# One call moved by one place in VectorE's order: the low part of a spectrum ahead of one low part of weights

## The chip, the cores and the metric

The program runs on one core of one Trainium2 chip. The metric is the device time of one execution in microseconds (us); lower is better. For the kernel before, three timed runs and one profiled execution are shown.

## The reference, cut to what matters

The program computes two transformer-like blocks, one behind the other, on 256 tokens of width 1024, all in fp32. The change lies in the second block, in its Hyena mixer, which convolves a sequence twice with a long filter and gates the result after each convolution:

```python
def long_conv_bidir(u, h_fwd, h_bwd, bias):
    ...
    U = jnp.fft.rfft(u.astype(jnp.float32), n=2 * L, axis=1)
    K = jnp.fft.rfft(k2, n=2 * L, axis=0)
    y = jnp.fft.irfft(U * K[None], n=2 * L, axis=1)[:, :L]
    ...
    for n in range(HY_ORDER):
        z = gates[n] * long_conv_bidir(z, filt[:, 0, n], filt[:, 1, n], bias[n])
```

Beside it stand the gate projections `h @ w_in` (the columns `gna` and `ghy`), which need nothing from the convolution.

## The kernel before, in words

**Numbers in two parts.** TensorE multiplies fp32r tiles. To keep fp32 accuracy, each operand is a high part (ScalarE copies the fp32 value into fp32r) and a low part (VectorE subtracts the high part from the value). A product is then three matmuls: high by high, low by high, high by low. This holds for weights (`wh`, `wl`), for the activations (`xh`, `xl`) and for the convolution's data (`zh`, `zl` ahead of the forward transform, `yh`, `yl` ahead of the inverse one).

**Weights.** All weights come as one stream of chunks of 1 MB, each of two *halves* of eight 128x128 tiles. SyncE loads chunks into three buffers `raw`, in order (`sync_load`, L375). A chunk may be loaded into a buffer only when VectorE has made the low parts of both halves of the chunk that was there; SyncE waits for those in turn. ScalarE makes the high part of a half (`casts`, L430, with `cast`, L420, which waits for the load), VectorE the low part (`rests`, L447, with `rest`, L441). Each of the sixteen gate projections, gate 0 to gate 15, uses one half; the half of gate 0 is the first of its chunk, so gates 6 and 7 share a chunk, 8 and 9 the next, and so on. The load of the chunk of gates 12 and 13 goes into the buffer of gates 6 and 7, so it is issued when gate 7's low part is there. That of gates 14 and 15 follows gate 9's low part, and that of the two halves behind gate 15 follows gate 11's. The high and low parts themselves lie in five slots here: the parts of gate g+5 go where those of gate g were, so ScalarE casts gate 12 behind the tanh of gate 7 (`gate_act`, L2410), and VectorE makes gate 7's low part in `rests(2)`, gate 8's in `rests(3)`, gate 9's in `rests(4)`, gate 10's in `rests(5)`, those of gates 11 and 12 in `rests(7)`.

**The convolution.** The channels go in two halves, (n, 0) and (n, 1), for each of the convolutions n = 0 and 1. One pass of (n, half) is:

- TensorE's forward transform, 12 matmuls (`fwd_pe`, L2462); they need `zl`, and the bank of the first six must have been read by the splitting of the pass before;
- ScalarE copies the odd bank out (`fwd_act`, L2479), and VectorE forms the sum and the difference of the banks (`fwd_split`, L2495);
- VectorE multiplies by the filter's spectrum and adds up (`fwd_products`, L2505; `fwd_sums`, L2516). The last two operations of `fwd_sums` are the two halves `w` of the product's spectrum, in the tile `a`;
- ScalarE makes the high part of each, `yh` (`fwd_high`, L2539), and VectorE the low part, `yl` (`fwd_low`, L2530, two operations; each waits for `w` and for `yh`);
- TensorE's inverse transform, 12 matmuls (`inv_pe`, L2550), which wait for both `yl`;
- for n = 0, VectorE gates the result (`z_next`, L2441), ScalarE and VectorE make its parts (`z_hi`, L2423; `z_lo`, L2432), and the next pass begins. For n = 1, ScalarE copies it out (`inv_act`, L2566) and TensorE transposes it (`hy_back`, L2573).

**The order.** Each engine works its instructions off in the order in which the program issues them; the order is written out by hand, for TensorE in `tail_pe` (L2627), for ScalarE in `tail_act` (L2656) and for VectorE in `tail_dve` (L2709). TensorE's begins

```python
        gate(2, 3, 4)
        self.inv_pe(P, 0, 0)
        gate(5, 6)
        self.inv_pe(P, 0, 1)
        gate(7)
        self.fwd_pe(P, 1, 0)
        gate(8)
        self.fwd_pe(P, 1, 1)
        gate(9, 10, 11)
        self.inv_pe(P, 1, 0)
        gate(12)
        self.hy_back(P, 0)
```

In ScalarE's order, `gate(7)` (the tanh of gate 7 and the cast of gate 12) stands ahead of `fwd_act(A, 1, 0)`.

Of the kernel before, what the change touches and what calls it, by code (L numbers as in the profile page):

```python
# [238 lines left out]
class Kernel:  # L239
# [207 lines left out]
    def rests(self, V, spent, late=False, most=None):  # L447

        W = self.W
        if late:  # L450
            V.spent, spent = spent, V.spent
        V.spent = max(V.spent, spent)
        end = W.halves if most is None else min(W.halves, V.next_half + most)
        while V.next_half < end:
            b = W.before[("half", V.next_half)]
            if b is not None and not (b[1] < spent if b[0] == "half" else b in V.over):
                break
            h = V.next_half
            if not self.on_pool(h):
                self.rest(V, ("half", h), self.S["w_lo"])  # L460
            V.next_half += 1
# [2247 lines left out]
    def tail_dve(self, V):  # L2709
        S, W = self.S, self.W  # L2710
        rests = lambda n: self.rests(V, W.spent(("gate", n)))
        self.fwd_split(V, 0, 1)
        self.fwd_products(V, 0, 1)
        self.fwd_sums(V, 0, 1)
        rests(2)
        self.fwd_low(V, 0, 1)
        self.z_next(V, 0)
        rests(3)
        self.z_lo(V, 1, 0)
        self.z_next(V, 1)  # L2720
        rests(4)
        self.z_lo(V, 1, 1)
        self.fwd_split(V, 1, 0)
        rests(5)
        self.fwd_products(V, 1, 0)
        self.fwd_sums(V, 1, 0)
        rests(7)
        self.fwd_low(V, 1, 0)
        self.fwd_split(V, 1, 1)
        rests(8)  # L2730
        self.fwd_products(V, 1, 1)
        self.rests(V, W.spent(("gate", 10)), most=1)
        self.fwd_sums(V, 1, 1)
        rests(10)
        self.fwd_low(V, 1, 1)
        rests(11)
        self.hy_gated(V, 0)
        rests(12)
        self.hy_lo(V, 0)
        rests(13)  # L2740
        rests(14)
        self.hy_gated(V, 1)
        for k in range(4):
            s = slice(512 * k, 512 * (k + 1))
            if k == 1:
                rests(15)
                self.hy_lo(V, 1)
            V.wait_ge(S["hy_a"], ("gate", 2 * k + 1))
            V.wait_ge(S["proj"], ("nao", 2 * k + 1))
            V.stt(self.SA[:, s], self.SA[:, s], 1.0, self.ps[self.bank[("nao", "twin", k)]][:, :], ALU.add,  # L2750
                  ALU.mult).then_inc(S["hy_v"], ("mna", k))
            if k < 3:
                self.rests(V, W.spent(("nao", 2 * k + 1)))
        V.wait_ge(S["out_a"], ("shift",))
        V.tt(self.pads()[:, :, 1:2], self.mod[:, 24:32].rearrange("p (d c) -> p d c", d=8),
             self.pads()[:, :, 0:1].bitcast(F32), ALU.subtract).then_inc(S["out_v"], ("shift",))

        def lower(k):
            s = slice(512 * k, 512 * (k + 1))
            V.wait_ge(S["hy_a"], ("mh", k))  # L2760
            V.tt(self.ML[:, s], self.merged(k), self.MH[:, s].bitcast(F32), ALU.subtract).then_inc(S["hy_v"], ("ml", k))

        self.rests(V, W.spent(("nao", 7)))
        for k in range(4):
            s, t = slice(512 * k, 512 * (k + 1)), self.merged(k)
            V.wait_ge(S["hy_a"], ("gate", 9 + 2 * k))
            V.wait_ge(S["proj"], ("hyo", 2 * k + 1))
            V.stt(t, self.SH[:, s], 1.0, self.ps[self.bank[("hyo", "twin", k)]][:, :], ALU.add,
                  ALU.mult).then_inc(S["hy_v"], ("mhy", k))
            V.wait_ge(S["hy_v"], ("mhy", k))  # L2770
            V.tt(t, t, self.SA[:, s], ALU.add).then_inc(S["hy_v"], ("m", k))
            if k:
                lower(k - 1)
                self.rests(V, W.spent(("hyo", 2 * k - 1)), most=1 if k == 3 else None)
        lower(3)
        V.over.add(("tail",))
        self.rests(V, W.spent(("hyo", 7)))
        add = lambda d: self.add_x(V, "mod", d, M0, TR, self.ps[self.bank[("out", d)]][:, :TR], ("out", d),
                                   self.small[:, 24 + d:25 + d])
        low = lambda d: self.norm_lo(V, "mod", d, M0, TR, self.small[:, 16 + d:17 + d], 258)  # L2780
        add(0), add(1), low(0), add(2), low(1)
        self.rests(V, W.spent(("out", 0)))
        low(2)
        for d in range(3, DT):
            self.rests(V, W.spent(("out", d - 2)))
            add(d)
            self.rests(V, W.spent(("out", d - 1)))
            low(d)
        self.rests(V, W.spent(("out", 7)))
        self.rsqrt_dve(V, "mod", self.R[1], self.ps[7][:, :TR], TR)  # L2790
# [328 lines left out]
```

## Time and profile before

| | before |
|---|---|
| timed runs, us | 1000.8, 1002.09, 1002.31 (median 1002.09) |
| profiled execution, us | 1005.83 |
| its span in the profile, us | 1004.0 |
| TensorE (PE) busy | 97% of the span |
| VectorE (DVE) busy | 82% |
| ScalarE (ACT) busy | 56% |
| granted TensorE clock, mean | 0.997 of full speed |

Busy time is an average over the whole program. In the stretch that the change touches, from 700 to 760 us, all of TensorE, VectorE and ScalarE depend on one another, so there the single instructions have to be read in order of time: when one starts, whether its engine sat idle ahead of it, and for whom it waited. Starts are counted from the beginning of the span. Two instructions that follow each other on VectorE or ScalarE overlap by about 0.1 us in the records, so the next one starts a little before the first one's end.

### The profile page before, as it was taken

How to read it: one execution, taken by the hardware profiler on the slowest of the kernel's cores; microseconds unless marked ns; L12 is line 12 of the kernel's file. 1: busy time of each engine (PE TensorE's matmuls, PEld its weight loads, DVE VectorE, ACT ScalarE, POOL GpSimd, SP SyncE). 2: the span in 40 equal slices, each digit the busy share in tenths (PEclk: the TensorE clock that was granted, in tenths of full speed). 3: DMA queues.
4: the chain of work that ended last, by engine and by line, in shares of the span. 5: the costliest groups of instructions: out<-in, count | busy, mean ns of one | idle time of the engine just before them, and what ended most of it. 6: DMA issues, size and time to landing. Idle time of an engine off the chain costs nothing.

```text
span 1004.0 us, 19347 instructions
## 1 busy us (share of the span) xinstructions
PE 973.0 (97%) x7884; PEld 951.9 (95%) x7884; DVE 822.7 (82%) x1376; ACT 562.5 (56%) x1051; POOL 102.8 (10%) x128
## 2 busy tenths in 40 slices
PE   7999999999999999999999999999999999999996
PEld 6999999999899989999999998889999999999996
DVE  7999798887999967999969967998998968767443
ACT  6756454445766756555545535666545556655432
POOL 4100000111000003002103301122000100000000
PEclk9999999999999999999999999999999999999998
DMA  9564657665433315998758813443345446555441
GB/s 281 224 253 166 241 200 237 236 232 204 154 141 105 127 63 209 344 324 298 272 173 296 322 52 134 143 142 110 123 165 211 172 154 221 211 170 197 144 162 42
DMA packets 33880, 192.17 MB, mean 191 GB/s; under 512 B 4976, under 2 KB 6272, under 8 KB 15104
## 3 DMA queue, kind: packets, MB, share of 16 engines
q1 hardware_dynamic: 23440, 157.36, 43.6%
q10 hardware_dynamic: 6912, 25.17, 7.4%
q0 software_dynamic: 3440, 8.42, 2.8%
q8 instruction: 62, 1.02, 0.4%
q14 instruction: 26, 0.21, 0.1%
HBM read 187.78 MB, written 3.15 MB: 190 GB/s over the span
## 4 chain that ended last, share of the span: by engine, by line
PE 77%; DVE 13%; ACT 6%; issue 2%; DMA 2%; SPq 0%; DVEq 0%; ACTq 0%
PE ps L93 76%; DVE wl L70 3%; ACT wh L67 2%; PE ps L96 1%; DMA raw<-w 1%; DVE a L70 1%; DVE b L70 1%; ACT u L67 1%; DMA cst<-cst 1%; DVE s L77 1%; DVE c L81 1%; DVE l L73 1%; ACT s L67 1%; DVE natl L70 0%; ACT a L67 0%
## 5 line engine op out<-in xcount | busy, mean ns | idle before, releaser
L70 DVE TENSOR_TENSOR wl<-raw,wh 128x1024 fp32r<-128x1024 f32 x283 | 343.8, 1230 | 16.1 <-ACT wh L67 15.8
L67 ACT ACTIVATE wh<-raw 128x1024 fp32r<-128x1024 f32 x286 | 295.9, 1049 | 23.5 <-PE ps L93 11.2
L93 PE MATMUL ps<-xh,wh 128*128 128x256 f32 (+1 forms) x992 | 279.7, 282 | 1.2 <-DVE xl L73 1.1
L93 PE MATMUL ps<-xh,wl 128*128 128x256 f32 (+1 forms) x992 | 278.5, 281 | 0.0
L93 PE MATMUL ps<-xl,wh 128*128 128x256 f32 x992 | 277.4, 280 | 0.0
L93 PE MATMUL ps<-xt,wh 128*128 128x272 f32 (+1 forms) x1120 | 217.4, 289 | 0.9 <-DVE wl L70 0.7
L93 PEld LDWEIGHTS ps<-xh,wh 128*128 128x128 f32 x992 | 188.2, 190 | 1.7 <-DVE xl L73 1.3
L93 PEld LDWEIGHTS ps<-xl,wh 128*128 128x128 f32 x992 | 187.1, 189 | 0.0
L93 PEld LDWEIGHTS ps<-xh,wl 128*128 128x128 f32 x992 | 186.7, 188 | 0.2
L93 PEld LDWEIGHTS ps<-xt,wh 128*128 128x128 f32 x1120 | 177.2, 188 | 2.2 <-issue 0.8
L93 PE MATMUL ps<-xt,wl 128*128 128x272 f32 (+1 forms) x560 | 160.1, 286 | 0.0
L93 PE MATMUL ps<-hl,wh 128*128 128x256 f32 (+1 forms) x528 | 149.1, 282 | 0.0
L93 PE MATMUL ps<-hh,wh 128*128 128x256 f32 (+1 forms) x528 | 149.0, 282 | 0.0
L93 PE MATMUL ps<-hh,wl 128*128 128x256 f32 (+1 forms) x528 | 149.0, 282 | 0.0
L93 PEld LDWEIGHTS ps<-xt,wl 128*128 128x128 f32 x560 | 105.7, 189 | 0.3
L93 PEld LDWEIGHTS ps<-hl,wh 128*128 128x128 f32 x528 | 100.0, 189 | 0.0
L93 PEld LDWEIGHTS ps<-hh,wh 128*128 128x128 f32 x528 | 99.5, 188 | 0.1
L93 PEld LDWEIGHTS ps<-hh,wl 128*128 128x128 f32 x528 | 99.1, 188 | 0.0
L70 POOL TENSOR_TENSOR acc<-acc,sq 128x256 f32<-128x256 f32 (+1 forms) x30 | 34.0, 1133 | 506.8 <-ACT sq L67 506.8
L67 ACT ACTIVATE hh<-fh 128x256 fp32r<-128x256 f32 (+1 forms) x66 | 27.9, 422 | 102.4 <-DVE fh L70 78.6
L67 ACT ACTIVATE sq<-x 128x256 f32<-128x256 f32 (+1 forms) x43 | 17.5, 417 | 84.3 <-DVE x L70 50.9
L84 DVE CUSTOM_DVE_ANT_0 ada<-ada,cb 128x1024 f32<-128x1024 f32 x42 | 55.9, 1330 | 0.1
(343 smaller groups left out, 1574.8 us busy)
## 6 DMA issues: line engine op xcount, KB each, us to landing
raw<-w SPq DMA_DIRECT2D x141, 1024.0 KB, 5.0
ada<-ada ACTq DMA_DIRECT2D x42, 512.0 KB, 4.5
cb<-ada ACTq DMA_DIRECT2D x6, 512.0 KB, 4.6
raw<-w SPq DMA_DIRECT2D x4, 512.0 KB, 6.5
spare<-w SPq DMA_DIRECT2D x2, 1024.0 KB, 9.3
spectra<-ev POOLq DMA_DIRECT2D x8, 256.0 KB, 3.7
skew<-rpb POOLq DMA_DIRECT2D x8, 192.0 KB, 3.5
x<-x POOLq DMA_DIRECT2D x2, 544.0 KB, 9.1
```

The source lines that it names most:

```text
L67: return Issued(self.e and self.e.activation(out, src, func, **kw))
L70: return Issued(self.e and self.e.tensor_tensor(out, a, b, op))
L73: return Issued(self.e and self.e.scalar_tensor_tensor(out=out, in0=in0, scalar=scalar, in1=in1, op0=op0, op1=op1))
L77: return Issued(self.e and self.e.tensor_scalar(out, src, s1, s2, op0=op0))
L81: return Issued(self.e and self.e.tensor_tensor_scan(out, a, b, 0.0, op0=ALU.add, op1=ALU.bypass))
L84: return Issued(self.e and self.e.tensor_tensor_reduce(out, a, b, scale, start, op0, op1, accum))
L93: return Issued(self.e and self.e.matmul(out, stat, mov, start=start, stop=stop))
L96: return Issued(self.e and self.e.transpose(out, src, ident))
```

## The change

In VectorE's order the two operations of `fwd_low` for (0, 1) are issued ahead of the low part of gate 7's weights instead of behind it. Nothing is added or removed, and no other engine's order changes. The calls that lie around it:

```diff
--- before.py
+++ after.py
@@ -2712,8 +2712,8 @@
         self.fwd_split(V, 0, 1)
         self.fwd_products(V, 0, 1)
         self.fwd_sums(V, 0, 1)
+        self.fwd_low(V, 0, 1)
         rests(2)
-        self.fwd_low(V, 0, 1)
         self.z_next(V, 0)
         rests(3)
         self.z_lo(V, 1, 0)
```

## Rows read from the trace of the kernel before

**Rows 1.** The profile's page, busy us of the engines

```profile
PE 973.0 (97%) x7884; PEld 951.9 (95%) x7884; DVE 822.7 (82%) x1376; ACT 562.5 (56%) x1051; POOL 102.8 (10%) x128
```

**Rows 2.** Waits, 704 to 760 us: us in total, times, longest us

```profile
ACT wh L67 <- DMA raw<-w: 2.7, 1, 2.7
...
PE ps L93 <- DVE yl L70: 0.9, 1, 0.9
...
PE ps L96 <- ACT a L67: 0.6, 1, 0.6
...
PEld ps L93 <- ACT sghy L67: 0.3, 1, 0.3
```

**Rows 3.** Waits of TensorE, 752 to 1004 us

```profile
PE ps L93 <- ACT sq L67: 0.6, 1, 0.6
```

**Rows 4.** The chain that ended last, 727 to 751 us: start, us, what

```profile
727.61 5.79 PE ps L93 x48
...
733.42 0.61 ACT a L67
...
741.72 1.15 DVE wl L70
...
742.93 6.11 DMA raw<-w
...
749.07 0.02 ACT wh L67
...
750.03 0.58 ACT a L67
...
750.75 0.63 PE ps L96 x4
```

**Rows 5.** VectorE in order of time: start, us, instruction, [idle before <-releaser]

```profile
723.92 1.29 DVE L70 TENSOR_TENSOR a<-b 128x512 f32<-128x512 f32 x2
725.13 1.22 DVE L70 TENSOR_TENSOR wl<-raw,wh 128x1024 fp32r<-128x1024 f32 x1
726.26 1.29 DVE L70 TENSOR_TENSOR yl<-a,yh 128x512 fp32r<-128x512 f32 x2
727.47 0.68 DVE L70 TENSOR_TENSOR z<-ps,g 128x512 f32<-128x512 f32 x1
728.07 1.22 DVE L70 TENSOR_TENSOR wl<-raw,wh 128x1024 fp32r<-128x1024 f32 x1
...
734.05 1.42 DVE L70 TENSOR_TENSOR a<-ps,a 128x512 f32<-128x512 f32 x2 [1.83 <-ACT a L67]
```

**Rows 6.** ScalarE in order of time, 724 to 733 us

```profile
725.24 0.63 ACT L67 ACTIVATE yh<-a 128x512 fp32r<-128x512 f32 x1
...
732.06 0.38 ACT L67 ACTIVATE sgna<-ps 128x256 f32<-128x256 f32 x1 [0.91 <-PE ps L93]
732.34 1.05 ACT L67 ACTIVATE wh<-raw 128x1024 fp32r<-128x1024 f32 x1
```

**Rows 7.** TensorE's matmuls and its weight loads (PEld), in order of time

```profile
727.61 0.39 PE L93 MATMUL ps<-yh,gh 128*128 128x256 f32 x1 [0.88 <-DVE yl L70]
...
735.94 0.28 PE L93 MATMUL ps<-zh,fh 128*128 128x256 f32 x1
...
727.60 0.19 PEld L93 LDWEIGHTS ps<-yh,gh 128*128 128x128 f32 x1 [1.07 <-DVE yl L70]
...
729.03 0.19 PEld L93 LDWEIGHTS ps<-xh,wh 128*128 128x128 f32 x1
```

**Rows 8.** SyncE's loads: issues, then us to landing (722:727, 700:765, 600:640, all)

```profile
726.42 0.33 SPq L99 DMA_DIRECT2D raw<-w  x1
...
DMA to landing us min/median/max: 4.8/4.8/4.8
...
DMA to landing us min/median/max: 4.8/4.9/6.1
...
DMA to landing us min/median/max: 4.8/4.8/7.1
...
DMA to landing us min/median/max: 3.4/5.0/11.7
```

## The prediction, made before the changed kernel was run

> **What bounds the kernel now.** I read the page first: TensorE is busy 97% of the span, VectorE 82% [rows 1]. A move on VectorE can only give back time in which TensorE waits for it, so the waits of the stretch come next. From 704 to 760 us TensorE stands three times: 0.9 us for `yl`, 0.3 us at a weight load, and 0.6 us at the transposes (L96) for ScalarE's `a` [rows 2]. From 752 us to the end it waits for 0.6 us in all, in the last norm [rows 3]. So whatever moves the transposes at 750.75 moves the end by as much, and nothing behind them gives it back.
>
> The chain says what moves them [rows 4]. The inverse transform (0, 1) starts at 727.61; 48 matmuls (inverse 12, gate 7 24, forward 12) run to 733.40; ScalarE copies the forward's bank out at 733.42; VectorE works through split, products and sums to gate 11's low part, which ends at 742.87; that frees a buffer, the load issued at 742.93 takes 6.11 us, and ScalarE, in order, casts at 749.07 and only then copies the inverse out at 750.03. Hence two questions: what the move does to 727.61, and whether that reaches 733.42.
>
> VectorE's order shows the part to be moved [rows 5]: the two `w` at 723.92, gate 7's low part at 725.13, the two `yl` at 726.26, `z` at 727.47. The first `yl` could start as soon as its `yh` is there. ScalarE's order shows the second `yh` from 725.24 to 725.87 [rows 6]; the first ends as the second starts, give or take 0.03 us.
>
> **The change, part by part.** *Removed from ahead of `yl`:* one 128x1024 subtraction. The two `w` end at 723.92 + 1.29 = 725.21. Now ScalarE sets the pace. The first `yl` starts at about 725.29. The second waits for the second `yh`, 725.87 + 0.03 (an ACT to DVE release as from 733.42 + 0.61 to 734.05 [rows 4, 5]) = 725.90. With 0.69 us of its own it ends at 726.59, against 726.26 + 1.29 = 727.55 before: 0.96 us earlier. TensorE's matmuls ahead of the inverse run out at 727.61 - 0.88 = 726.73 by the records [rows 7], and the first weight load may go 0.05 us behind `yl`, at 726.64. **The inverse starts 0.96 us earlier** and the wait of 0.9 us is gone.
>
> *Moved behind `yl`:* gate 7's low part. VectorE's start to start for a 128x512 subtraction ahead of another operation is 728.07 - 727.47 = 0.60 us [rows 5], so it starts at 725.90 + 0.60 = 726.50, not 725.13: **1.37 us later**, ending at 727.72. Three things wait for it.
>
> (a) TensorE's gate 7. The inverse takes 729.03 - 727.60 = 1.43 us [rows 7], so gate 7's first weight load comes at 726.64 + 1.43 = 728.07; the low part is there at 727.72 + 0.05. No wait, with 0.3 us to spare.
>
> (b) VectorE itself. The swapped operations fill the same time but for 0.17 us of standing for `yh`: `z` goes from 727.47 to 727.64, and all up to the last `zl` moves by that. The 1.83 us in which VectorE stands at 734.05 [rows 5] covers it.
>
> (c) SyncE. The load of gates 12 and 13 waits for exactly this low part: it was issued at 726.42 [rows 8], 0.07 us behind its end at 725.13 + 1.22 = 726.35. Now: 727.72 + 0.07 = 727.79. This same load took 4.8 us to land [rows 8]: 731.22 before, 1.1 us ahead of the cast of gate 12 at 732.34 [rows 6], and **732.59 after**. TensorE is 0.96 us ahead, so gate 7's tanh comes at about 731.2 and ScalarE would cast gate 12 at 731.5. It has to stand there until 732.59 + 0.03 = 732.62, and the copy of the forward's bank is queued behind. In the chain such a copy starts 750.03 - 749.07 = 0.96 us behind the cast [rows 4]: 732.62 + 0.96 = **733.58, against 733.42. That is 0.16 us later than before**, although TensorE has the bank ready at 732.44. This is the step on which the forecast rests: the gain on TensorE is real and is eaten by a load that the same move delays.
>
> From there on each step repeats the chain, 0.16 us later. VectorE's split moves from 734.05 to 734.21, its end from 735.47 to 735.63. The second forward transform, at 735.94 before [rows 7], is reached at 734.98 but needs the split: 735.68. So here TensorE gives back 0.70 of its 0.96 us. Gate 11's low part ends at 743.03 instead of 742.87; there TensorE stood 0.3 us before [rows 2] and now stands about 0.26 + 0.16 = 0.4 us longer, which gives back the rest. The load behind it goes out at 743.09, and with 6.11 us as before the transposes start at 750.91. What that last load takes is not the change's doing: at the 4.9 us of its neighbours [rows 8] its wait for ScalarE at the transposes would be gone, in either kernel, and gate 11's low part, still 0.16 us later, would set the end.
>
> The sum is -0.96 (inverse) +0.96 (given back at the split and at gate 11) +0.16 (ScalarE's cast behind the load) = **+0.16 us**, on the profiled execution 1005.83 + 0.16 = 1005.99. The timed runs lie 3.7 us below that one; nothing in the term depends on that difference, so it goes on their median: 1002.09 + 0.16 = 1002.25, rounded to 1002.2.
>
> The unknown price is the landing of the delayed load. Each 0.1 us of it is 0.1 us at the end, down to a floor of -0.96, where the cast no longer holds ScalarE (landing 3.7 us and less). Ends from rows: 3.4 us, the shortest of the trace, gives -0.96; 7.1 us, the longest in the stretch from 600 to 640 us, gives +2.46 [rows 8]. I take 4.8, since it is this very load's figure and the smallest and nearly the median of the stretch. Two loads beside it, of 4.9, would make it +0.26.
>
> The Trainium skill (DMA: Bandwidth & Descriptors, section Anatomy of one DMA) fits a DMA that GpSimd issues with about 2.0 us plus its bytes by 436 GB/s. As an estimate from that page, 1 MB lands in 4.4 us, which would make the sum -0.24 us instead of +0.16; the trace's 4.8 decides here, and both are no change.
>
> **The rivals.** *A, the gain stays.* ScalarE is not held by the cast, because the load lands within 3.7 us. Then 733.42 becomes 732.46, the chain moves by -0.96 and so does the end: 1002.09 - 0.96 = 1001.1. For it: TensorE is the busiest engine and its one wait for `yl` goes. Against it: none of the loads from 700 to 765 us landed in under 4.8 us [rows 8].
>
> *B, the load lands late.* It is one mechanism: gates 12 and 13's load, issued 1.37 us later, runs into whatever made the load at 742.93 take 6.11 us [rows 4]. Before, a landing of up to 5.9 us cost nothing (732.34 - 726.42); now each tenth over 4.64 us costs. At 6.1 us it is 4.8's +0.16 plus 1.3: 1003.6. It passes 0.2% (2.0 us, about what a measurement of this kernel can tell from no change) only from 6.65 us of landing; at 7.1 us the time is 1002.09 + 2.46 = 1004.6. For it: one load of eight here took 6.1. Against it: over 6.65 is rare, and it would have to fall on this load in most runs.
>
> *C, the move does nothing.* If the second `yh` came later than reckoned, ScalarE and not VectorE's order would set `yl`, at its old time. For that `yh` would have to be 0.96 us late, and it is on record at 725.24 [rows 6]. Then only the load's delay would be left, +0.16 as well: 1002.2.
>
> **How the numbers follow.** The forecast, between -0.3 and +0.5 us, gets 0.74; rival A, or part of it, 0.10; rival B at 6.1 us or so 0.08, and past 0.2% 0.04; C 0.02; 0.02 is for what I don't see, on either side. All but B's far end and the unseen lie within 0.2% of 1002.09. B's far end and half of the unseen make slower 0.05; the other half, and A where the measurement adds as much again, make faster 0.03; the same gets 0.92. The timed runs of one kernel lie 1.5 us apart, so a median may be off by some 0.5 us: the range goes from A's 1001.1 less 0.5 to B's 1003.6 (its own spread is in the two in ten left out), 1000.6 to 1003.6.
>
> **What would show it.** In the changed kernel's trace: `yl` at about 725.3 and 725.9; no wait of TensorE for `yl`; the load issued at 727.8; a new wait of ScalarE's `wh` for the load of about 1.1 us ahead of 732.6; the copy `a` at 733.6; new waits of TensorE of about 0.7 us near 735 and 0.7 us near 743. The prediction is wrong if that wait of ScalarE's isn't there, or if 733.42 moves by more than 0.4 us either way. If the end moves and 733.42 does not, it is the late load behind gate 11, not the change.

## The result, and the profile after

The changed kernel takes 1004.0 us (median of 19 runs, 1002.01 to 1005.3) against 1001.89 us for the kernel before (19 runs, 1000.49 to 1003.23). The ratio is 1.0019, with a 95% interval of 1.0012 to 1.0025: **1.9 us slower, between 1.2 and 2.5**. Forecast were 1002.2 us and a range from 1000.6 to 1003.6.

The profiled execution of the changed kernel took 1002.4 us, its span is 1000.6 us. That is less than the span of before, and it says nothing: the two executions differ by 3.6 us before they come to the change at all (the last section says where). So times are counted here from a common mark, the start of the first `w` of (0, 1) on VectorE, at 723.92 us before [rows 5] and at 720.31 us after. VectorE of the changed kernel in order of time:

```profile
720.31 1.29 DVE L70 TENSOR_TENSOR a<-b 128x512 f32<-128x512 f32 x2
721.77 1.29 DVE L70 TENSOR_TENSOR yl<-a,yh 128x512 fp32r<-128x512 f32 x2 [0.17 <-ACT yh L67]
722.99 1.22 DVE L70 TENSOR_TENSOR wl<-raw,wh 128x1024 fp32r<-128x1024 f32 x1
724.12 0.68 DVE L70 TENSOR_TENSOR z<-ps,g 128x512 f32<-128x512 f32 x1
...
731.80 1.42 DVE L70 TENSOR_TENSOR a<-ps,a 128x512 f32<-128x512 f32 x2 [2.93 <-ACT a L67]
```

The order is the one meant. `yl` ends at +2.75 instead of +3.63, 0.88 us earlier; gate 7's low part starts at +2.68 instead of +1.21, 1.47 us later. But VectorE then stands 2.93 us for ScalarE's copy `a`, not 1.83 [rows 5]. ScalarE shows why:

```profile
727.71 0.37 ACT L67 ACTIVATE sgna<-ps 128x256 f32<-128x256 f32 x1
730.23 1.06 ACT L67 ACTIVATE wh<-raw 128x1024 fp32r<-128x1024 f32 x1 [2.15 <-DMA raw<-w]
731.20 0.57 ACT L67 ACTIVATE a<-ps 128x512 f32<-128x512 f32 x1
```

The tanh of gate 7 is done at 728.08, and the cast of gate 12 waits 2.15 us for its load. Before, there was nothing to wait for at this place [rows 6]. The copy of the forward's bank stands behind the cast and starts at +10.89 instead of +9.50, 1.39 us later. SyncE in order of time has the load's issue:

```profile
724.28 0.33 SPq L99 DMA_DIRECT2D raw<-w  x1
```

and the view of the tile `raw` what it took to land:

```profile
DMA to landing us min/median/max: 5.9/5.9/5.9
```

It went out at +3.97 instead of +2.50 and took 5.9 us instead of 4.8 [rows 8]. The chain that ended last now runs from gate 7's low part through this load, where before it ran over TensorE [rows 4]:

```profile
723.07 1.15 DVE wl L70
...
724.28 5.92 DMA raw<-w
730.21 0.02 issue
730.23 1.06 ACT wh L67
731.29 0.49 ACT a L67
...
739.47 1.15 DVE wl L70
...
740.68 6.27 DMA raw<-w
...
747.94 0.59 ACT a L67
...
748.66 0.63 PE ps L96 x4
```

From the copy on it is the chain of before, link by link. The transposes come at 748.66 - 720.31 = +28.35, against 750.75 - 723.92 = +26.83: **1.52 us later**, 1.36 from the first load and 0.16 from the second, which took 6.27 us instead of 6.11. The waits of TensorE in the changed kernel (716 to 757 us: us in total, times, longest):

```profile
PE ps L93 <- DVE a L70: 1.7, 1, 1.7
PE ps L96 <- ACT a L67: 0.7, 1, 0.7
PE ps L93 <- DVE wl L70: 0.3, 1, 0.3
```

The 0.9 us for `yl` [rows 2] is gone, and 1.7 us stand in its place, ahead of the second forward transform, whose bank the delayed split has not yet read.

### The profile page after: what moved, and what is told of

It reads as the page before. It is cut to its first block, busy times and chain, and to the rows that moved or that the text cites. A ratio compares the mean times of both kernels' runs of the same rounds, so it can differ in the third digit from the quotient of the medians.

```text
span 1000.6 us, 19347 instructions
## 1 busy us (share of the span) xinstructions
PE 968.3 (97%) x7884; PEld 947.3 (95%) x7884; DVE 822.1 (82%) x1376; ACT 562.7 (56%) x1051; POOL 104.9 (10%) x128
## 3 DMA queue, kind: packets, MB, share of 16 engines
q8 instruction: 62, 1.02, 0.4%
## 4 chain that ended last, share of the span: by engine, by line
PE 76%; DVE 13%; ACT 6%; DMA 2%; issue 2%; SPq 0%; DVEq 0%; ACTq 0%
PE ps L93 75%; DVE wl L70 3%; ACT wh L67 2%; DMA raw<-w 2%; PE ps L96 1%; DVE a L70 1%; DVE b L70 1%; ACT u L67 1%; DVE c L81 1%; DVE s L77 1%; DMA cst<-cst 1%; DVE l L73 1%; ACT s L67 1%; DVE natl L70 0%; DVE s L84 0%
```

## The experiments

T1 is the theory that the loss is the load of gates 12 and 13, delayed by the move, through ScalarE's order. R is the rival that VectorE's new order makes it by itself, C that one long landing was chance. All times with a plus sign count from the first `w` of (0, 1). The table collects what the traces show; "late load" is the one behind gate 11's low part, and a fetch is a packet of 16 KB on the instruction queue q8, in us behind the load's issue ("none": none from the issue to the landing). The last column is the time from the first `w` of (0, 1) to the end of the span; in the two traces marked *, TensorE's pace late in the program was another one (last section), which makes this figure some 1.3 us smaller.

| kernel | load issued | took | fetch | copy | late load took | fetch | transposes | end of span |
|---|---|---|---|---|---|---|---|---|
| before | +2.51 | 4.8 | 4.4 | +9.50 | 6.1 | 1.5 | +26.8 | +280.1 |
| before, again | +2.51 | 4.7 | 4.2 | +9.50 | 6.1 | 3.0 | +26.9 | +280.1 |
| after | +3.97 | 5.9 | 2.5 | +10.9 | 6.3 | 2.9 | +28.4 | +280.3 * |
| after, again | +3.98 | 6.0 | 2.6 | +11.0 | 6.3 | 2.9 | +28.4 | +281.7 |
| after, copy first | +3.97 | 6.1 | 2.7 | +8.63 | 6.0 | 2.9 | +25.9 | +279.1 |
| before, load late | +3.72 | 4.9 | 4.5 | +9.64 | 6.5 | 3.4 | +27.3 | +280.6 |
| before, load later | +5.46 | 4.8 | none | +11.3 | 6.5 | 1.5 | +29.0 | +282.2 |
| after, shifted | +3.97 | 4.9 | none | +9.82 | 4.8 | none | +26.3 | +280.1 |
| before, shifted | +2.50 | 4.8 | none | +9.51 | 4.9 | none | +26.0 | +279.9 |
| after, both first | +3.97 | 6.9 | 2.3 | +8.65 | 6.2 | 2.8 | +25.4 | +277.7 * |
| before, both first | +2.51 | 4.8 | 4.3 | +9.50 | 6.4 | 1.5 | +26.0 | +279.9 |
| after, both first, shifted | +3.97 | 4.7 | none | +8.63 | 4.8 | none | +25.3 | +278.9 |

**The copy ahead of the cast.** In the changed kernel, ScalarE copies the forward's bank out before it casts gate 12:

```diff
-        gate(7)
+        self.gate_act(A, 7, False)
         self.fwd_act(A, 1, 0)
+        self.casts(A, W.spent(("gate", 7)))
```

with `gate_act` making its casts only if its third argument is true.

> The changed kernel with one more move: in ScalarE's order the copy of the forward's bank (fwd_act for (1, 0)) stands ahead of the cast of gate 12. Theory T1 (the loss is the load of gates 12 and 13, issued later, which holds ScalarE at the cast with the copy queued behind): the copy no longer waits for the load and follows TensorE, about 2.3 us earlier than in the changed kernel, so this kernel comes out about 1.0 us faster than the kernel before (1000.9 us against 1001.9) and about 2.5 us faster than the changed one; the wait of ScalarE for the load may stay, but nothing of the chain is behind it. Rival R (the loss is VectorE's own new order: its standing for yh, or gate 7's low part made late): it stays at about 1.9 us slower than before.

Measured: 1000.96 us against 1001.6, ratio 0.9998 (0.9985 to 1.0011). ScalarE in order of time:

```profile
732.10 0.60 ACT L67 ACTIVATE a<-ps 128x512 f32<-128x512 f32 x1 [0.86 <-PE ps L93]
733.53 1.06 ACT L67 ACTIVATE wh<-raw 128x1024 fp32r<-128x1024 f32 x1 [0.84 <-DMA raw<-w]
```

The load took 6.1 us and the cast still waits for it, but the copy now follows TensorE, at +8.63. The transposes are at +25.9, 0.97 us ahead of those of before and 2.5 us ahead of the changed kernel's, and the end of the span is 1.0 us ahead: the whole gain that the move of `yl` makes on TensorE reaches the end as soon as ScalarE's order does not put the load in its way. R falls: it had this kernel 1.9 us slower than before, and the timed runs have it 0.2 us faster, between 1.5 us faster and 1.1 us slower. They alone would not have shown the gain of 1 us, since their interval is 2.6 us wide; that is read from the trace. Of the 0.97 us, 0.88 are TensorE's lead at the second forward transform and 0.09 the late load's, which took 6.02 us instead of 6.11.

**The load alone, late.** The kernel before, VectorE's order untouched, with one more wait of SyncE's:

```diff
+        if x == ("w", 101):
+            D.wait_ge(self.S["hy_v"], ("yl", 0, 1, 1))
```

> The kernel before with one more wait: SyncE issues the load of gates 12 and 13 only when both yl of (0, 1) are there, 1.2 us later than before, with VectorE's order as before. T1: the load lands at about 732.4 us if it takes 4.8 us, which costs nothing, and at about 733.5 if TensorE's instruction fetch falls into it as it did in the changed kernel; then the copy moves from 733.4 to 734.5 and the time by +1.1 us, to 1003.0. R: VectorE's order is that of before, so no change, 1001.9.

Measured: 1001.86 us against 1001.6, ratio 1.0003 (0.9987 to 1.0019). The load took 4.9 us, the copy came at +9.64 and so cost 0.14 us; another 0.4 us at the transposes is the late load's, which took 6.5 us here. It is T1's harmless branch, and thus no proof: R expected as much. The fetch came 4.5 us behind the issue, when the load was all but in. So the same load was held back further, until gate 8's low part:

```diff
+        if x == ("w", 101):
+            D.wait_ge(self.low_signal(198), ("half", 198))
```

> The kernel before with VectorE's order untouched and the load of gates 12 and 13 held back further: SyncE issues it when gate 8's low part is there, at +5.44 instead of +2.51 (times from the start of the first w of (0, 1)). T1 (the load alone, through ScalarE's order, makes the loss): with 4.8 us it lands at +10.2, the copy of the forward's bank moves from +9.5 to +11.2, the transposes from +26.8 to +28.5, and the time is 1.7 us over that of the kernel before; with a fetch in it (6 us) the copy is at +12.4. R (VectorE's new order makes the loss): this order is that of before, so the copy stays at +9.5 and the time at that of before.

Measured: 1004.29 us against 1001.78, ratio **1.0022** (1.0011 to 1.0033). ScalarE in order of time:

```profile
729.11 1.06 ACT L67 ACTIVATE wh<-raw 128x1024 fp32r<-128x1024 f32 x1 [1.76 <-DMA raw<-w]
730.08 0.58 ACT L67 ACTIVATE a<-ps 128x512 f32<-128x512 f32 x1
```

Its load took 4.8 us. The copy is at 730.08 - 718.82 = +11.3, as expected, and the transposes at +29.0, 2.1 us late (1.76 from the copy, 0.4 from the late load's 6.5 us). VectorE's order is that of before. A late load by itself makes the loss of the changed kernel, and more.

**The fetch.** That leaves why the load took 5.9 us. The page has a queue that I had passed over: q8, kind instruction, 62 packets, 1.02 MB. The DMA view of the changed kernel, from the issue to 728.9 us, when the load should have been in:

```profile
DMA packets 142, 1.05 MB, mean 228 GB/s; under 512 B 15, under 2 KB 15, under 8 KB 15
## 3 DMA queue, kind: packets, MB, share of 16 engines
q1 hardware_dynamic: 141, 1.03, 63.2%
q8 instruction: 1, 0.02, 1.3%
```

Each of the 16 engines ends its share of a load with a packet of 4 B. By 728.9 there are 15 of them, and one packet of q8 is among the load's. It takes 1.3% of the 16 engines' 4.6 us, which is 0.96 us, close to the 1.1 us by which this load is longer. The sixteenth comes about 1.1 us behind the others (the view from 729.3 to 730.2 us):

```profile
DMA packets 18, 0.14 MB, mean 155 GB/s; under 512 B 1, under 2 KB 1, under 8 KB 1
```

In the kernel before, the load's data from 726.4 to 730.7 us has no q8 packet beside it:

```profile
q1 hardware_dynamic: 133, 1.05, 71.7%
issues: line engine op xcount, KB each, median us to landing
raw<-w SPq DMA_DIRECT2D x1, 1024.0 KB, 4.8
```

To test it, 60 waits that are long satisfied were put into TensorE's stream, far ahead, where they cost nothing, in either kernel:

```diff
+            if name[:2] == ("up", 1) and P.e is not None and t % 4 == 3 and P.spent < 60:
+                P.spent += 1
+                P.e.wait_ge(self.low_signal(h).sem, self.low_signal(h).at[("half", h)])
+                P.e.wait_ge(self.S["ld_fz"].sem, self.S["ld_fz"].at[("load",)])
```

> The changed kernel with 60 more instructions in TensorE's stream, waits that are long satisfied, spread over the up projections of layer 1, where they cost nothing. They move each of TensorE's instruction fetches of 16 KB behind them about 3.4 us earlier against the work. T1 in its strong form (the load takes 5.9 us because one such fetch, at 726.8 us in the changed kernel's trace, holds one of the 16 DMA engines in the midst of it): the fetch falls ahead of the load, the load lands in 4.8 us, the copy comes 1.1 us earlier than in the changed kernel, and the later load of 6.3 us falls to about 4.9 as well. The time against the same shift of the kernel before is +0.2 us instead of +1.9. If the long landing has another cause, the load still takes 5.9 us and the difference stays at +1.4 to +1.9.

> The kernel before with the same 60 satisfied waits in TensorE's stream: the partner of the shifted changed kernel. T1: the later load, 6.1 us before, lands in 4.8 to 4.9 us, TensorE's wait of 0.6 us at the transposes goes, and the time falls by 0.6 to 0.8 us against the kernel before, to 1001.2. The load of gates 12 and 13 may take 6 us here, which costs nothing since the cast of gate 12 comes 5.9 us behind its issue. If fetches have nothing to do with landings, both loads stay as before and the time too.

Measured: the changed kernel shifted takes 1000.92 us (ratio 0.9992, 0.9981 to 1.0004), the kernel before shifted 1001.66 us (1.0007, 0.9995 to 1.0019), both against 1001.6. ScalarE of the shifted changed kernel, in order of time:

```profile
727.55 1.06 ACT L67 ACTIVATE wh<-raw 128x1024 fp32r<-128x1024 f32 x1 [1.09 <-DMA raw<-w]
728.52 0.58 ACT L67 ACTIVATE a<-ps 128x512 f32<-128x512 f32 x1
```

and the landings of its load of gates 12 and 13 and of the late load:

```profile
DMA to landing us min/median/max: 4.9/4.9/4.9
...
DMA to landing us min/median/max: 4.8/4.8/4.8
```

The fetch next to the first load moved 5.2 us earlier in the changed kernel and 5.8 in the one before, not 3.4. That it moved says whose it is: only TensorE's stream was changed. Their number fits: 62 packets for the 7884 matmuls and 7884 weight loads of the page is one for every 254 of these, so a fetch comes at nearly fixed places of TensorE's stream. Both loads fell, 5.9 to 4.9 and 6.3 to 4.8 us. ScalarE's wait is the 1.09 us that the prediction had. Against its partner the shifted changed kernel is 0.31 us later at the copy and 0.30 at the transposes: the forecast's +0.16, a little larger; at the end of the span it is 0.24 us.

The expectation for the kernel before, 0.6 to 0.8 us faster, was missed: its transposes came 0.8 us earlier, the end of its span only 0.2 us, and the timed runs show nothing (1001.66 against 1001.6). TensorE's waits of that kernel from 748 us on, with a new one beside the 0.6 us of [rows 3], and VectorE ahead of it, show where the gain went:

```profile
PE ps L93 <- DVE yl L70: 0.3, 1, 0.3
```

```profile
750.11 1.22 DVE L70 TENSOR_TENSOR wl<-raw,wh 128x1024 fp32r<-128x1024 f32 x1
751.25 1.28 DVE L70 TENSOR_TENSOR yl<-a,yh 128x512 fp32r<-128x512 f32 x2
```

The inverse of (1, 1) now waits for `yl`, which again stands behind a low part of weights in VectorE's order. So the prediction's premise that nothing behind the transposes gives back what they gain holds only while the late load delays them. The changed kernel gained 1.6 us at the end of the span by the shift (281.7 to 280.1), against 2.0 at the transposes; its ratio to before went from 1.0019 to 0.9992, some 2.7 us, with intervals of over 1 us each.

The table makes the rule of it: of its 24 loads, the 13 into which a fetch fell 1.5 to 3.4 us behind the issue took 5.9 to 6.9 us; the 11 others, with a fetch 4.2 us or more behind the issue or none, took 4.7 to 4.9. A load that the table leaves out bears it out: the one issued at +37 to +40 takes 5.4 to 6.0 us in the nine traces without the shift, with a fetch 1.0 to 1.7 us behind its issue, and 4.8 to 5.1 in the three with it. It is not the only reason for a long landing: six loads from 690 to 770 us took 5.3 to 6.0 us without a fetch, five of them issued while the load ahead was still landing.

The Trainium skill (DMA: Bandwidth & Descriptors, Queues, rings and completion order) says that each DMA engine takes turns between the queue rows, a packet at a time, and that the write which raises the semaphore lands only behind every earlier write of its engine. The trace agrees: 15 completion packets are on time, and the one of a single engine is 1.1 us late.

**The same programs once more.**

> The changed kernel once more, for a second profile of the same program. Times counted from the start of the first w of (0, 1). T1 (TensorE's instruction fetch meets the delayed load in this order): the load of gates 12 and 13 is issued at +3.97 and takes 5.8 to 6.1 us again, the copy is at +10.8, the transposes at +28 (26.8 in the kernel before), and the time is 1.4 to 1.9 us over that of the kernel before. Rival C (the one long landing was chance, not bound to the order): it takes 4.8 to 5.0 us here, the copy is at +9.8 and the transposes at +27.

> The kernel before once more, for a second profile of the same program. T1: the load of gates 12 and 13 is issued at +2.5, takes 4.8 to 4.9 us, and the fetch comes behind its landing or too late to matter (+6.9 to +8.3); the copy is at +9.5. The later load may take 4.9 or 6.1 us, so the transposes are at +26.0 to +27.4. C: a long landing of the first load is as likely here as in the changed kernel.

Measured: the changed kernel 1004.08 us against 1002.09, ratio 1.0016 (1.0 to 1.0031); the kernel before against itself 1003.46 us, ratio 1.0013 (0.9989 to 1.0036), whose interval is wide enough to hold either. The traces are sharper. The changed kernel's second trace, packets from 724.8 to 729.2 us:

```profile
DMA packets 136, 1.03 MB, mean 235 GB/s; under 512 B 11, under 2 KB 11, under 8 KB 11
...
q8 instruction: 1, 0.02, 1.3%
```

The load took 6.0 us. The fetch meets it in all four traces of kernels with the change and without the shift, and in none of the five with neither. C falls. From the common mark to the end of the span the second trace of the changed kernel has 281.69 us, those of before 280.10 both times: +1.59.

**Both copies first.** The late load can be taken out of the chain in the same way: ScalarE copies the last inverse out ahead of the cast that waits for it.

```diff
-        gate(9, 10, 11)
+        gate(9, 10)
+        self.gate_act(A, 11, False)
         self.inv_act(A, 0)
+        self.casts(A, W.spent(("gate", 11)))
```

> The changed kernel with two moves in ScalarE's order: the copy of the forward's bank ahead of the cast of gate 12, and the copy of the last inverse ahead of the cast behind gate 11 (the one that waits for the late load). T1: neither load can hold the chain. The transposes come at +25.1 against +26.8 in the kernel before, so 1.7 us faster than before, about 1000.1 us if the kernel before takes 1001.8, and 0.8 us faster than the kernel with the first move alone. If the copies are held by something else, the transposes stay at +25.9 or later.

> The kernel before with the same two moves in ScalarE's order. T1: the first move changes nothing here, since the load lands 1.1 us ahead of its cast and the copy waits for TensorE anyway; the second takes the late load out of the chain, so the transposes come at +26.0 against +26.8: 0.8 us faster than the kernel before, and 1.0 us slower than the changed kernel with both moves. Rival R (the changed order of VectorE is worth nothing by itself): both kernels with the two moves come out alike.

> The changed kernel with both of ScalarE's copies moved ahead of their casts, and with the 60 satisfied waits in TensorE's stream that move its fetches off the two loads. T1: the loads take 4.8 to 5.0 us instead of 6.2 to 6.9; since nothing of the chain stands behind them any more, that is worth little: the transposes at +25.1, against +25.4 without the shift, and the time within 0.5 us of that of the kernel with both moves, about 1000 us. If a load still held the chain in that kernel, the transposes would come 1 us or more earlier here.

Measured: with the change 1000.12 us against 1002.09, ratio **0.9981** (0.9966 to 0.9997); without it 1001.2 us, 0.9993 (0.9978 to 1.0008); with change and shift 1000.37 us against 1001.78, **0.9986** (0.9975 to 0.9996). ScalarE of the first, in order of time:

```profile
742.16 0.60 ACT L67 ACTIVATE a<-ps 128x512 f32<-128x512 f32 x1 [1.10 <-PE ps L93]
```

The copy of the last inverse waits for TensorE alone, at +22.8 instead of +26.1. The transposes are at +25.4, +26.0 and +25.3: 1.4, 0.8 and 1.6 us ahead of before. With the shift the loads take 4.7 and 4.8 us instead of 6.9 and 6.2, which is worth 0.1 us, so a load no longer decides. The change with both of ScalarE's moves beats both kernels, in the timed runs by 1.9 us against before (between 0.3 and 3.4), with the shift by 1.4.

At the end of the span the gain is smaller than at the transposes. Without the change it is 0.25 us: the inverse of (1, 1) waits 0.3 us for `yl`, as in the kernel before, shifted. With change and shift it is 1.2 us, and that wait is 0.2 us. So the expected 1.7 us was not reached, and that the timed 1000.12 us is the expected 1000.1 is in part luck. On top of the two moves the change is worth 0.86 us at the second forward transform (+11.17 against +12.03), 0.65 at the transposes and 0.86 again at the inverse of (1, 1) (+31.54 against +32.40). The 1.0 us expected was too much: TensorE's wait for `yl`, all that the move can give back, is 0.88 us in these traces [rows 7]. Where the 0.2 us in between went stays open; TensorE's matmuls show no wait of over 0.1 us from 715 to 760 us.

## Why the prediction was wrong

- **The inverse 0.96 us earlier:** right in kind, somewhat too much. `yl` ended 0.88 us earlier; the first `yl` stood 0.17 us for ScalarE, where the forecast had 0.08. The inverse itself started 0.73 us earlier (+2.96 against +3.69; 0.88 in the trace with the copy first). By the prediction's own row TensorE's matmuls run out at 726.73, so 0.88 us was the most that could come of it. None of it decided the time.
- **Gate 7's low part 1.37 us later, TensorE not held by it:** right, 1.47 us, and TensorE has no wait there.
- **VectorE's own order covered:** right; its wait of 1.83 us only grew.
- **The load issued 1.37 us later, ScalarE held at the cast with the copy behind:** right in mechanism. The wait is there, at its place.
- **"This same load took 4.8 us to land" as the price after the move:** this is the step that failed. It took 5.9 us (6.0 in the second trace). The term +0.16 came out as +1.39 at the copy. The figure was taken from the load at its old time, and the move had changed just that, its time against TensorE's stream: before, the fetch came 4.2 to 4.4 us behind the issue, when the data were in; after, 2.5 us behind it, amid the data. With the fetch moved away the term is +0.3.
- **TensorE's lead given back at the split and at gate 11:** right, in the places named, with 1.7 us ahead of the second forward transform where 0.7 was forecast.
- **The late load's 6.11 us kept:** 6.27, +0.16.
- **Nothing behind the transposes gives anything back:** right for a delay, and for the 1.0 us of the copy first. Where the late load no longer holds the transposes, nearly 0.6 of their 0.8 us is given back until the end, 0.3 of it in the wait of the inverse of (1, 1) for `yl`.
- **The rivals and the range:** A and C are out, since ScalarE was held at the cast and `yl` came earlier. Rival B had the right mechanism, its price (1003.6 at 6.1 us) and its point of decision, but 0.08 of the chance; and it counted the one long landing of eight as a draw by lot. It is no lot: that load took 6.0 to 6.5 us in all nine traces without the shift, and 4.8 to 4.9 us in the three with it. The range ended at B's 1003.6 and had no room for the 0.4 us by which the timed runs lie above it; the trace gives 1.5 to 1.6 us of the measured 1.9, within its interval of 1.2 to 2.5.

## What to carry to other kernels

An operation that is moved back delays every load which waits for its buffer, and an engine that works in order puts everything behind the first user of that load; look for what stands there, and if something of the chain does, move it ahead of the user. A load's landing time is not a constant that moves along with it: see on the DMA queues which instruction fetches run when, and price a moved load by the long landing as well, since one fetch in its midst made it some 1 to 2 us longer here. Where executions of one program differ by more than the effect, two traces read from a common mark show it to 0.1 us. Read them to the end of the span too: what is gained at one point can be given back at the next wait behind it.

## What the runs showed of the hardware that was not expected

**Fetches meet loads at the same place every time.** TensorE's stream comes in by packets of 16 KB on q8, 62 in the program. Their times against the work differed by up to 1.6 us between traces of one order, but the long landing stayed with its load. Sixty instructions of padding removed the two of the table, at no cost that the timed runs show (the kernel before, 1.0007, 0.9995 to 1.0019).

**TensorE has two paces at full clock.** The 3.6 us by which the two spans differ ahead of the change come from TensorE's pace. From 490 to 515 us of before and of after (busy us and count of PE, PEld, DVE, ACT, POOL, then the granted clock, the DMA share and GB/s):

```profile
490.00:515.00 25.00, 25.00 (x215) 25.00 (x214) 18.75 (x31) 10.00 (x15) 0.00 (x0) 1.00 0.68 233
```

```profile
490.00:515.00 25.00, 25.00 (x220) 24.95 (x219) 18.99 (x34) 12.02 (x17) 0.00 (x0) 1.00 0.66 224
```

TensorE is busy throughout at a granted clock of 1.00 in both, and does 215 matmuls in the one and 220 in the other. From 440 to 490 us it does 427 and 444. From 540 to 565 us it is the changed kernel's trace that has the slower pace, 214 against 223, which gives a part of the difference back. Of the twelve traces two did 215 here (before, and the changed kernel with the copy first), and their first `w` of (0, 1) is at 723.9 and 723.5 us; the ten others did 219 or 220, and theirs lie between 718.7 and 721.0. Late in the program, from 935 to 975 us, the changed kernel's two traces differ in the same way (from 855 to 930 us the other way round, 626 matmuls in the first and 632 in the second), the first

```profile
935.00:975.00 40.00, 40.00 (x355) 40.00 (x355) 18.75 (x19) 16.43 (x23) 2.96 (x4) 1.00 0.43 159
```

and the second

```profile
935.00:975.00 40.00, 40.00 (x342) 40.00 (x341) 18.76 (x19) 16.43 (x23) 2.96 (x4) 1.00 0.43 159
```

Both traces of before have 342. From the common mark to the end the changed kernel's first trace has 280.27 us and its second 281.69, so the first shows only 0.2 us of the loss at its end and the second 1.6. The pace changes between executions of one program; what sets it was not tried and stays open.
